# Expert weights through a ring of eight 2 MB places instead of six fixed ones, and three small loads moved to the end

## The reference

```python
h = rmsnorm(x, norm2_g[l]) * (1 + scale2) + shift2
x = x + gate2 * hier_moe(h, ...)      # then y = rmsnorm(x, final_norm_g)

# inside hier_moe: 16 experts, each token goes to 2 of them
hid = silu(t @ w_gate[e]) * (t @ w_up[e])     # 2048 -> 512
hid = hid * gates[..., e]
out += hid @ w_down[e]                        # 512 -> 2048
```

## Time and profile before

| | us |
|---|---|
| median of 3 runs | 1317.91 |
| lowest, highest | 1315.68, 1320.37 |
| the profiled execution, its own time | 1317.38 |
| its span in the profile | 1315.7 |
| mean granted clock of PE, share of full speed | 0.967 |

### The profile page before, as it was taken

The page is one execution under the profiler, slowest core; times in us unless marked ns, Lnnn a source line. Parts: engine busy times, 40 slices in busy tenths (PEclk is TensorE's granted clock), DMA queues, the critical chain, the costliest instruction groups (busy, mean ns, idle before and its releaser), DMA issues.

```text
span 1315.7 us, 15030 instructions
## 1 busy us (share of the span) xinstructions
PE 1184.9 (90%) x6080; PEld 633.1 (48%) x6081; DVE 297.3 (23%) x660; ACT 200.2 (15%) x393; POOL 70.7 (5%) x120
## 2 busy tenths in 40 slices
PE   4989899999999999999999399879988998899883
PEld 1445556545455444545555245544544454445540
DVE  2101302212122223103113611211111111111128
ACT  3111201113112123011111101110111011101102
POOL 1003000010000000010000000000000000000000
PEclk9999999999999999999999599999998999899996
DMA  9999876878656457593632588999999999999982
GB/s 330 387 388 367 259 300 268 319 287 323 260 229 276 195 224 282 207 342 136 237 136 80 186 324 343 397 410 420 382 418 410 409 369 424 404 408 376 419 326 92
DMA packets 82698, 406.20 MB, mean 309 GB/s; under 512 B 6363, under 2 KB 8651, under 8 KB 53565
## 3 DMA queue, kind: packets, MB, share of 16 engines
q1 hardware_dynamic: 73888, 371.21, 72.2%
q0 software_dynamic: 7392, 28.51, 6.0%
q10 hardware_dynamic: 1376, 5.88, 1.2%
HBM read 394.32 MB, written 21.94 MB: 316 GB/s over the span
## 4 chain that ended last, share of the span: by engine, by line
PE 72%; DMA 21%; DVE 4%; issue 1%; ACT 1%; SPq 1%; POOLq 0%; DVEq 0%; ACTq 0%
PE bank L828 21%; DMA arena<-in_w_gate_dram 12%; PE bank L1230 9%; PE bank L1227 6%; PE bank L913 6%; PE bank L832 5%; PE bank L823 4%; PE bank L1253 4%; DMA arena<-in_w_ada_dram 4%; PE bank L864 3%; PE bank L1250 2%; DMA arena<-in_w_down_dram 2%; PE bank L844 2%; DMA arena<-in_w_up_dram 2%; PE bank L879 1%
## 5 line engine op out<-in xcount | busy, mean ns | idle before, releaser
L828 PE MATMUL bank<-arena 128*128 128x512 f32 x640 | 288.3, 601 | 0.0
L1227 PE MATMUL bank<-arena 128*64 128x256 f32 x1536 | 176.2, 387 | 27.8 <-DMA arena<-in_w_gate_dram 16.9
L828 PEld LDWEIGHTS bank<-arena 128*128 128x128 f32 x640 | 118.7, 191 | 135.6 <-issue 134.6
L1227 PEld LDWEIGHTS bank<-arena 128*64 128x64 f32 x1536 | 110.9, 139 | 97.1 <-DMA arena<-in_w_gate_dram 22.2
L1230 PE MATMUL bank<-arena 128*128 128x512 f32 x256 | 114.1, 607 | 9.2 <-DMA arena<-in_w_gate_dram 8.1
L1250 PE MATMUL bank<-arena 128*64 128x512 f32 x384 | 85.0, 595 | 6.0 <-DVE arena L1795 6.0
L913 PE MATMUL bank<-arena 128*128 128x320 f32 x320 | 87.7, 433 | 0.0
L1230 PEld LDWEIGHTS bank<-arena 128*128 128x128 f32 x256 | 49.3, 194 | 73.4 <-issue 62.7
L1792 DVE SCALAR_TENSOR_TENSOR arena<-bank,arena 128x512 f32<-128x512 f32 x16 | 12.0, 751 | 309.0 <-PE bank L1227 190.1
L913 PEld LDWEIGHTS bank<-arena 128*128 128x128 f32 x320 | 60.1, 189 | 28.3 <-issue 3.2
L832 PE MATMUL bank<-arena 128*64 128x256 f32 x640 | 73.5, 382 | 0.0
(11 more groups left out here) (344 smaller groups left out, 857.1 us busy)
## 6 DMA issues: line engine op xcount, KB each, us to landing
arena<-in_w_ada_dram SPq DMA_DIRECT2D x48, 2048.0 KB, 14.3
arena<-in_w_gate_dram SPq DMA_DIRECT2D x32, 2048.0 KB, 21.3
arena<-in_w_up_dram SPq DMA_DIRECT2D x32, 2048.0 KB, 21.6
arena<-in_w_down_dram SPq DMA_DIRECT2D x32, 2048.0 KB, 21.1
arena<-in_w_in_dram SPq DMA_DIRECT2D x16, 2048.0 KB, 8.1
arena<-in_w_out_dram SPq DMA_DIRECT2D x8, 2048.0 KB, 11.3
arena<-in_w_in_dram SPq DMA_DIRECT2D x4, 1536.0 KB, 17.4
arena<-mod_final POOLq DMA_DIRECT2D x6, 1024.0 KB, 18.7
```

Source lines behind the costliest of these rows:

```text
L828: return mm(bank[:, :], lhsT=xT_[:, t, OFF[j]:OFF[j] + P], rhs=w, start=start, stop=stop)
L1227: last = mm(PB[bank][64 * h:64 * h + 64, 0:HALF], lhsT=XeT[:, t0 + t, 0:64], rhs=slots_w[slot][:, t, HALF * h:HALF * h + HALF], start=star ...
```

## The change

- There are eight places: the six of before, F0 at the range HT (where g2b was), and F1 at SA - 2048 to SA + 2048. For F1 the arena is laid out anew: the tables cT, modrow, wdt and wr, used by then, move to the end of the small tables just ahead of SA, and x moves behind SA.
- Chunk n = 6 i + k of visit i goes to `ring[n % 8]`, in the order E0, E1, A0, A1, W0, W1, F0, F1. The semaphores stay six, one for each kind of chunk.
- On SP, chunk n waits until PE has used chunk n - 8, and until chunk n - 6, which counts on the same semaphore, has landed. Chunk 6 waits for the second norm, for the first gather and for chunk 0; chunk 7 for the storing of the first block of h2 and for chunk 1.
- All 16 visits are written out on SP. On PE, visits 1 to 15 are written out, each in both forms; a loop is left for passes that these inputs don't have.
- g2b and gfin go to W0 and W1's first half, and SP issues their loads, after the result rows of blocks 0 and 1 and before those of block 2, once the last visit's up product is done. `routed` rises to 1 as soon as the scatter of the visit before the last has landed, and no longer waits for the last chunk. g2b for the second stream is loaded for 64 partitions.

```diff
-        slot_off = [0, SLOT, 2 * SLOT, 3 * SLOT, EB, EB + SLOT]
+        slot_off = [0, SLOT, 2 * SLOT, 3 * SLOT, EB, EB + SLOT, HT, SA - D]
+        ring = (E0, E1, A0, A1, W0, W1, F0, F1)
+        kinds = ((E0, "g", 0), (E1, "g", 1), (A0, "u", 0), (A1, "u", 1), (W0, "d", 0), (W1, "d", 1))
+        uses_before = {E0: 0, E1: 0, A0: 22, A1: 22, W0: 15, W1: 15}
+        def places(i):
+            n = 6 * min(i, NE - 1)
+            return [ring[(n + k) % 8] for k in range(6)]
-        g2b, gfin = at(HT, 2, D), at(SA, D)
+        g2b, gfin = at(0, 2, D), at(SLOT, D)
...
-            for g in range(4):
-                expert(4 * g, g)
-            with sp.Fori(1, 4) as a:
-                for g in range(4):
-                    expert(a + 4 * g, 4 * a + g)
+            for i in range(NE):
+                for k, (count, kind, half) in enumerate(kinds):
+                    n = 6 * i + k
+                    if n >= 8:
+                        before_i, before_k = (n - 8) // 6, (n - 8) % 6
+                        used = kinds[before_k][0]
+                        sp.wait_ge(slot_used[used], before_i + 1 + uses_before[used])
+                        if before_i < i - 1 or before_k < k:
+                            sp.wait_ge(slot_in[count], 16 * (i + uses_before[count]))
+                    elif ring[n] in (F0, F1):
+                        if ring[n] == F0:
+                            sp.wait_ge(h2_ready, 3)
+                            sp.wait_ge(Xe_in, 16)
+                            sp.wait_ge(slot_in[E0], 16)
+                        else:
+                            sp.wait_ge(h2_stored[0], 32)
+                            sp.wait_ge(slot_in[E1], 16)
+                    elif uses_before[count]:
+                        sp.wait_ge(slot_used[count], uses_before[count])
+                    chunk(places(i)[k], count, kind, half, i // 4 + 4 * (i % 4))
...
             sp.wait_ge(routed, 1)
             for j in range(3):
+                if j == 2:
+                    sp.wait_ge(routed, 2)
+                    for b in range(2):
+                        n = DEC if b else P
+                        sp.dma_start(g2b[0:n, b, :], modf_d[3, b].partition_broadcast(n)).then_inc(tail_in, 16)
+                    sp.dma_start(gfin, final_norm_g.partition_broadcast(P)).then_inc(tail_in, 16)
...
+            pool.sem_inc(routed, 1)
+            pool.wait_ge(slot_used[A1], last_visit + 23)
+            pool.sem_inc(routed, 1)
             pool.wait_ge(Xe_in, 16 * last_visit + 32)
-            pool.wait_ge(slot_used[A1], last_visit + 23)
-            pool.wait_ge(slot_in[W1], 16 * last_visit + 256)
             pool.sem_inc(routed, 1)
...
-            for b in range(2):
-                act.dma_start(g2b[:, b, :], modf_d[3, b].partition_broadcast(P)).then_inc(tail_in, 16)
-            act.dma_start(gfin, final_norm_g.partition_broadcast(P)).then_inc(tail_in, 16)
...
-            with pe.Fori(1, last_visit + 1) as i:
-                ...
+            for i in range(1, NE):
+                visit(i, places(i))
+            with pe.If(last_visit > NE - 1):
+                with pe.Fori(NE, last_visit + 1) as i:
+                    visit(i, places(NE))
```

More of the change, by code:

```diff
@@ L404, in _ @@
                         for g in range(4):
-                            expert(a + 4 * g, NE * p + 4 * a + g)
+                            for k, (count, kind, half) in enumerate(kinds):
+                                sp.wait_ge(slot_used[count], NE * p + 4 * a + g + uses_before[count])
+                                chunk(places(NE)[k], count, kind, half, a + 4 * g)
             sp.wait_ge(routed, 1)
             for j in range(3):
+                if j == 2:
[4 more added lines that the diff above has]
+                    sp.dma_start(gfin, final_norm_g.partition_broadcast(P)).then_inc(tail_in, 16)
                 for c in range(2):
@@ L1214, in transpose_rows, with expert @@
                     last.then_inc(XTp, 1)
-            def expert(i, few):
-                for bank, s0, s1, base in ((0, E0, E1, 1), (1, A0, A1, 23)):
-                    for slot, t0 in ((s0, 0), (s1, 8)):
-                        arrived(slot, i + base)
+            def expert(i, few, place):
+                for bank, first, base in ((0, 0, 1), (1, 2, 23)):
+                    for k, t0 in ((first, 0), (first + 1, 8)):
+                        count, slot = kinds[k][0], place[k]
+                        arrived(count, i + base)
                         for t in range(8):
@@ L1242, in expert @@
                 pe.wait_ge(XeT_s, 2 * i + 4)
-                for slot, t0 in ((W0, 0), (W1, 2)):
-                    arrived(slot, i + 16)
+                for k, t0 in ((4, 0), (5, 2)):
+                    count, slot = kinds[k][0], place[k]
+                    arrived(count, i + 16)
                     for t in range(t0, t0 + 2):
@@ L1254, in expert, with visit @@
                                           start=(t == 0), stop=(t == 3))
-                    last.then_inc(slot_used[slot], 1)
+                    last.then_inc(slot_used[count], 1)
+            def visit(i, place):
+                few = pe.value_load(small_pe[0:1, slice(i, i + 1) if isinstance(i, int) else bass.ds(i, 1)].bitcast(I32), min_val=0, max_val=1)
+                pe.wait_ge(XeT_v, 2 * i + 2)
+                pe.wait_ge(XeT_s, 2 * i + 2)
+                pe.wait_ge(hid_ready, i + 1)
+                with pe.If(few > 0):
+                    expert(i, True, place)
+                with pe.Else():
+                    expert(i, False, place)
             slot_info(0, 0)
@@ L1268, in first_expert @@
                 pe.wait_ge(hid_ready, 1)
-                expert(0, few)
+                expert(0, few, places(0))
             with pe.If(few > 0):
```

50 lines of the change are left out of this document (19 added, 31 removed).

## The result

Before 1319.02 us, after 1323.18 us (medians of nine runs each); ratio 1.0038, interval 1.0020 to 1.0057. The kernel became slower by 0.4%, where 1300 was forecast. The profiled execution of after has a span of 1319.1 us, against 1315.7.

What follows compares the result with a forecast made beforehand. DMA bounds few visits, PE wide ones, and six slots can't store the wide visit's surplus. DVE's first sum at 806.5 + 434.5 + 16.6 + 4.6 + 1.5 = 1263.7, 17.3 us sooner, gives 1317.4 - 17.3 = 1300 us; range 1287 to 1313.

Steps and rivals of the forecast that it cites:

- Head start: Visit 0: chunks 6 and 7 are requested 12.3 us before today's first request, putting the stream two chunks ahead from 806.5.
- Rate of the stream: Weight stream after 806.5: the 82 remaining chunks, 180.6 MB, move at 415.6 GB/s and take 434.5 us.
- 4.6 us for the end of the weights: Last 22.7 us of the weights: 4.6 us lost as DMA engines finish apart, kept behind the tail loads.
- own low end of 451 us: Weight stream: at today's mean of 5.50 us each, the 82 remaining chunks take 451 us.
- rival A: Weight stream: two chunks gained once, dips behind wide visits are small packets, not empty queues; 1312.3 us, chance 0.20.
- The mean of today's saturated stretches over a cycle: Weight stream: 27.7 us at 427 and 68.8 us at 411 GB/s average 415.6 GB/s, taken as the new rate.
- Jumps at nothing: PE's written-out visits: jumps over the unused form cost nothing, as the loop's first pass showed no gap at 823.11.
- Rival C: PE's visits: jumps wait for code, 3.2 us per few visit, 4.1 per wide one; 1320.4 us, chance 0.06.
- Tail loads: Before DVE's first sum: 6.81 MB behind the last weights at 411 GB/s take 16.6 us, against 12.3 today.
- 1.5 us for code: PE's written-out visits: 38 instruction packets, 0.63 MB, take 1.5 us of transfer.
- The failure named beforehand: End of the kernel: the prediction would be wrong if DVE waits for more than 20 us behind the last weights.
- The sum: DVE's first sum begins at 1263.7 against 1281.0, 17.3 us sooner, with the same instructions afterwards, so 1300 us.

Runs made afterwards that it cites:

- e12: e6 with POOL's gathers (but the first) and all its scatters replaced by transfers of 64 bytes: 1273.99 us.
- e14: e6 with the gathers kept and each scatter replaced by a direct transfer of 64 bytes: 1308.16 us.
- e1: The kernel before, six slots and its own tail, with only PE's loop written out, visits 1 to 15 each in both forms: 1333.03 us.
- e6: The kernel after with each visit in only the form it takes with these inputs, so no branch in PE's visits: 1323.5 us.
- e3: The kernel after without the three tail loads (gate2 and final norm row) and without DVE's wait for them: 1314.89 us.
- e11: The kernel after with first-stream gate2 loaded between rows of j = 0 and 1, and DVE waiting for each tail load only where used: 1316.15 us.
- e2: The kernel before with only the three tail loads taken from ACT and put on SP ahead of the rows of j = 2: 1329.68 us.
- e9: The kernel after with one more wait on POOL: rows and tail loads are requested only when the last weights have landed: 1324.89 us.
- e4: The kernel after with the second gate2 load going to all 128 partitions, not 64: 1322.61 us.
- e5: The kernel after with the three tail loads reading distinct rows in place of one row for all partitions: 1321.36 us.
- e15: e6 with each indirect transfer replaced by a direct one with half the rows on the same queue: 1321.00 us.
- e13: e6 with each indirect transfer replaced by a direct one of full size on the same queue: 1347.01 us.

## Why the prediction was wrong, by its own steps

**Head start: right.** Two requests at 745.25 (forecast 749); visit 4 was 119.5 us behind visit 0 (870.62 - 751.13), against 129.2 before: 9.7 us, two chunks, as forecast. It was to start "without a wait for its gate chunk": so it did, but it met a gap of 2.45 us for code, and one of 5.06 inside it.

**Rate of the stream: wrong, the largest term.** The 82 chunks were to take 434.5 us and took 453.0; with the forecast's 4.6 us for the end of the weights, which belong to this stretch, it is 439.1 against 453.0, 13.9 us. That is 5.52 us a chunk, today's pace and the forecast's own low end of 451 us: the ring gave its two chunks once, as rival A said, and no better rate. "The mean of today's saturated stretches over a cycle" took the 427 GB/s of the wide visits into the mean, as if a fuller queue would bring the average there. The dips did rise (384 and 361 to 410 and 414), but to the 411 of a few stretch at full share, not above; the third did not; and in the stretch from 870 to 1205 the rate went only from 401 to 407. The warning was in the earlier trace rows: 411 GB/s at a share of 1.01 is a full machine, and I had read it as such under rival A. e12 and e14 show what holds it there: 424 GB/s without rows, 410 with the gathers alone.

**Jumps at nothing: wrong as a step, small in the sum.** The evidence, no gap at 823.11, was taken in the loop of before, and this is what the change dissolves. Rival C had the mechanism; its price of 3.2 us for each few visit was wrong (one gap of 2.8 us in after, one of 0.9 in e1), and 4.1 for a wide one was low (up to 9.8). Six slots pay it with 13.4 us (e1); with eight it lies beside the bound (e6). Nor is a gap its length alone: behind the one of 5.06 us, 62 products took 29.51 us at a mean granted clock of 0.91, where visit 0's 64 took 27.73 at 1.00. Not seen by the forecast at all: the exit from the visits is such a jump too. 4.46 us stand ahead of L1328, where its counterpart in before followed the last products (end 1272.94) without a gap:

```profile
1272.87 0.64 PE L1291 MATMUL bank<-arena 128*128 128x128 f32 x3
```

In after the late tail loads hide this gap too; in e3 and e11, where DVE waits for PE, it is on the path (4.8 and 4.9 us).

The Trainium skill (Runtime: NRT & Kernel Launch, Instruction fetch mechanics) says that a taken branch out of the resident pages stops until its target is fetched; the gaps of 2.5 to 9.8 us, which went with the branches in e6, agree. It adds that kernels therefore prefer full unrolling; here the rolled loop, both forms inside it, ran without these gaps, and the unrolled one cost 1.0%. The measurement decides.

**Tail loads: wrong.** "At the 411 GB/s of a few stretch 16.6 us" (18.1 with the 1.5 us for code) was the forecast from the last chunk's landing to DVE's start; it was 1284.57 - 1256.6 = 28.0 us. In e2 the same bytes took 20.7 us. The early request, which the forecast counted as a merit, put the loads behind what was still in flight (10 us of the 32, e9) and won nothing, and the last of it crawls at 274 and 128 GB/s. The failure named beforehand, DVE waiting for more than 20 us behind the last weights, came true. Why it crawls is open; e3, e4 and e5 show that it is neither these loads, nor the partition count, nor the repeated row.

**The sum.** DVE's start was forecast at 1263.7 and came at 1284.57, 20.9 us later; and as visit 0 happened to begin 3.0 us sooner, the forecast is short by 23.9 us. The stream has 13.9 of them and the stretch behind the last landing 9.9. Had the loads been in time, PE would have been next, 8.1 us sooner (e3: 1276.44), with the exit jump in its path. The ring gave 8.5 us up to the last products, and the tail loads and the exit jump took more than that: rival A with a part of C behind it, and a tail that no rival held. That the result lies so near to no change is a sum of these opposites.

## What to carry to other kernels

Here a stretch with a DMA share of 1.00 had its rate already, at 410 GB/s as at 424: price a deeper ring by the surplus that it stores once, and look for what makes packets longer. When a loop is written out, look for jumps over a form that the old loop held, and at the exit first, where no stream of weights covers them. A load moved behind the last weights is read from when it is requested to when all in front of it has landed; give each its own semaphore, so that the first consumer waits for the one it needs (e11_split: its first sum 8.3 us sooner, its median 7.0 us lower than that of after).

## What the runs showed of the hardware

- Gathered rows on POOL's queue cost the stream more than their bytes: 4.6 MB of them cost at least 29.1 us (495.7 against 466.6), where the bytes are 11, and the rate fell from 424 to 410 GB/s at a full share. Rows beyond that cost about their bytes (e14 to e6, e15 to e13). The indirect form moves only the rows that its table names, and is no dearer than the direct one for nearly the same bytes (1323.5 and 1321.0 us).
- A jump over 240 records showed no gap at the jump itself (2.8 us once, 12 products behind it), one over 370 took 2.5 to 9.8 us, in visit 4 of after with 5.1 us more two products on. Why the same jump differs this much is open; the longest was at visit 12 in both kernels (8.74 and 9.83).
- What is requested while the last weights are in flight moves slowly at the end: 274 and 128 GB/s with a share of 1.03 and 0.78 in after, 220 at 0.97 in e3 without the tail loads; requested behind the last landing it is 229 GB/s at 1.05 in e9, and in e2 the norm row took only 17.6 us. In e12, where no rows move beside the weights, it still took 31.3 us. The cause is open; e4 and e5 exclude the partition count and the repeated row.
